# Start of a hybrid decoder block: input requested first, meta tokens over another queue, first query panel by units

## Chip, cores and metric

One core of one Trainium2 chip runs the whole block. The metric is the device time of one execution in microseconds. Three runs of the kernel before took 1568.35, 1568.96 and 1569.6 us.

## The reference, cut to what matters

```python
h = jnp.concatenate([meta, x], axis=1)         # 16 meta tokens + 256 tokens, D_MODEL = 2048
u = rmsnorm(h, attn_norm_w[l])
z = u @ w_in[l]                                # 12368 columns
hq, hf, hi, hg, aq, ak, av, iq, ik, iw, ga, gb = split_cols(z, IN_SIZES)
y_h = hgrn2_mix(hq, hf, hi, hg, lbs[l], hgrn_norm_w[l])
y_a = dsa_mix(aq, ak, av, iq, rmsnorm(ik, idx_k_norm_w[l]), iw, topk)
m = sigmoid(ga) * (y_h @ w_branch_hgrn[l]) + sigmoid(gb) * (y_a @ w_branch_dsa[l])
h = h + m @ w_out[l]
u = rmsnorm(h, ffn_norm_w[l])
a = causal_dwconv(u @ w_ffn_gate[l], ffn_conv_w[l], ffn_conv_b[l])
h = h + (silu(a) * (u @ w_ffn_up[l])) @ w_ffn_down[l]
return rmsnorm(h, final_norm_w)[:, N_META:]
```

All of it is float32.

## The kernel before, in words

Every projection is computed as products of a rounded part (`_hi`) and a remainder (`_lo`): hi x hi, hi x lo and lo x hi. The weights come in panels of 2048 x 256 float32 (2 MB) into two slots, `raw[0]` and `raw[1]`. A panel holds two units of 128 columns. For each unit n ScalarE rounds (`round_unit`, L1241, into `w_hi[n % 4]`, increments `hi_ready`), VectorE subtracts (`rest`, L1569, into `w_lo[n % 4]`, increments `lo_ready`), and TensorE multiplies when `lo_ready` reaches n + 1. SyncE asks for a panel when the remainders of the panel two before are done (`load`). All engines run programs written out by hand, in order, and are tied by semaphores alone.

The change concerns the first 25 us. Unit 0 and 1 are the 80 columns of the indexer's keys and head weights (`KEYS`), units 2 to 9 its queries. In order of the engines:

- SyncE's queue asks for the norm weights (8 KB), the 16 meta rows (128 KB, into partitions 112 to 127 of `x_tok[0]`), then x's left half, the first half of the keys' rows, x's right half, the second half of the keys' rows, the first query panel in two requests of 1 MB (8 of the 16 row blocks each), ten vectors, and the panel of units 4 and 5.
- TensorE warms up on `ones`, turns the norm weights, turns the meta rows (16 transposes, L733), and turns x: 16 column blocks k of two transposes each, into one of seven banks (`turn_x`). The keys' products (L763, L764, L767) run block by block between the turns: `keys_high(k)` waits for `ul_ready` k + 1, `turn_x(k + 7)` follows, and `keys_low(k)` uses `w_lo[0]` once `key_lo` is set (from k = 2 on). Then comes unit 2, in halves: 8 rounded products (L810), 8 products with the remainder (L814), and the rest. Unit 3 follows, with the product that spreads the roots of the token norms (L797, `spread_roots`) after its ninth step and the turn of the vectors after its thirteenth.
- ScalarE squares the meta rows (L1287), rounds the meta tokens' u (L1298), rounds x's turned blocks times the norm weights (`round_x`, L1294), and between the third and fourth of them the first half of the keys (L1302). After the sixteenth it rounds unit 2 in two halves (L1305, L1307; the second waits for the whole panel), rounds unit 3, squares x's first 128 tokens (L1309), and takes the roots (L1311).
- VectorE clears 112 rows of `x_tok[0]` (L1579), weights the turned meta tokens (L1588, four products), and takes the remainders of u (L1601, `rest_x` L1597), with the remainder of the keys' first half between the fourth and fifth (L1605). Then unit 2's remainders (L1609, L1613), unit 3's (L1569), x's second square (L1616), and later the diagonals (L1631) for which L797 waits.
- GpSimd makes `ident`, `ones` and `eps` and does the second half of the keys: rounding L540, remainder L542.

Of the kernel before, what the change touches and what calls it, by code (L numbers as in the profile page):

```python
# [15 lines left out]
F32 = mybir.dt.float32  # L16
F32R = mybir.dt.float32r
ACT = mybir.ActivationFunctionType
# [78 lines left out]
def hybrid_block(nc, x, meta_tokens, attn_norm_w, w_in, hgrn_lb_logits, hgrn_norm_w, idx_k_norm_w,  # L97
# [3 lines left out]
    with ctx:  # L101
# [33 lines left out]
        junk2 = at("junk2", R[0] + 32768, [P, D])  # L135
        vec_rows = at("vec_rows", R[7], [P, 3, P])
        diag = at("diag", R[4] + 6144, [P, 3 * P])
        u_meta = at("u_meta", R[4] + 7680, [P, KT, META])
        x_rs = at("x_rs", R[7] + 7680, [P, T])
# [115 lines left out]
        x_half = [sem(f"x_half{a}") for a in range(2)]  # L255
# [4 lines left out]
        query_in = sem("query_in")  # L260
        key_hi = sem("key_hi")
        key_lo = sem("key_lo")
        meta_turned = sem("meta_turned")
        meta_weighted = sem("meta_weighted")
        meta_rounded = sem("meta_rounded")
# [109 lines left out]
        conv_ready = sem("conv_ready")  # L375
        silu_ready = sem("silu_ready")
        hid_ready = sem("hid_ready")
# [64 lines left out]
        def _(sp):  # L442
# [252 lines left out]
        def _(pe):  # L695
# [29 lines left out]
            pe.wait_ge(consts, 4)  # L725
            warm_up(3)
# [5 lines left out]
            def turn(out, t, k):  # L732
                return nc.tensor.transpose(out, x_tok[t][:, P * k:P * k + P], ident[:])  # L733
# [1343 lines left out]
```

## Time and profile before

| | us |
|---|---|
| median of three runs | 1568.96 |
| lowest, highest | 1568.35, 1569.6 |
| the profiled execution | 1567.8 |
| its span, first to last instruction | 1566.1 |
| TensorE busy | 1554.6 (99%) |
| VectorE busy | 1013.6 (65%) |
| ScalarE busy | 706.1 (45%) |
| GpSimd busy | 141.6 (9%) |
| moved by DMA | 294.62 MB, 188 GB/s on average |

Times in rows are microseconds from the span's start, durations follow. PE is TensorE, DVE VectorE, ACT ScalarE, POOL GpSimd, SP SyncE; a q behind it is its queue. `[0.57 <-DMA x_tok]` behind a row says how long the engine was idle ahead of it and what ended that. Ends of matmuls are modelled, so their starts tell more than their durations.

### The profile page before, as it was taken

The page shows a single profiled execution, that of the slowest core. Times are in us where ns is not written, and L with a number is a line of the kernel's source. Part 1 is how long each engine was busy: PE and PEld are TensorE (multiplying, and loading weights), DVE is VectorE, ACT ScalarE, POOL GpSimd, SP SyncE. Part 2 cuts the span into 40 slices and gives each one's busy share as a digit, 9 for nine tenths or more (in the row PEclk, how much of TensorE's full clock was granted, in tenths as well). Part 3 has the DMA queues.
Part 4 walks back from the last instruction along what each step waited for, and adds up shares of the span by engine and source line. Part 5 has one row for each costly group of instructions (what it writes and reads, how often), then busy time and mean ns, then how long its engine had stood idle before and what let it go on. Part 6 is the DMA issues. An engine that isn't in the chain of part 4 may idle for free.

```text
span 1566.1 us, 28179 instructions
## 1 busy us (share of the span) xinstructions
PE 1554.6 (99%) x11644; PEld 1464.0 (93%) x11644; DVE 1013.6 (65%) x1222; ACT 706.1 (45%) x717; POOL 141.6 (9%) x225
## 2 busy tenths in 40 slices
PE   9999999999999999999999999999999999999998
PEld 7899999999999999999999999998889999998886
DVE  6655888843365666786777777775446777776453
ACT  6433555543433355653445545553333333344342
POOL 1000140000000002247620000000000000000000
PEclk9999999999999999999999999999999999999999
DMA  7765555655565554587877556564556565656551
GB/s 239 231 198 161 161 168 186 197 184 170 184 204 164 162 162 137 180 269 199 231 219 242 190 177 198 161 213 163 213 183 193 173 202 165 203 167 227 177 213 54
DMA packets 264523, 294.62 MB, mean 188 GB/s; under 512 B 23945, under 2 KB 249450, under 8 KB 264306
## 3 DMA queue, kind: packets, MB, share of 16 engines
q1 hardware_dynamic: 238434, 278.78, 54.8%
q0 software_dynamic: 4000, 8.45, 1.9%
q10 hardware_dynamic: 22016, 6.33, 1.7%
q8 instruction: 56, 0.92, 0.2%
q14 instruction: 17, 0.14, 0.0%
HBM read 285.12 MB, written 8.42 MB: 187 GB/s over the span
## 4 chain that ended last, share of the span: by engine, by line
PE 98%; DMA 1%; DVE 1%; SPq 0%; ACT 0%; issue 0%; DVEq 0%
PE ps L701 21%; PE ps L702 20%; PE ps L703 20%; PE ps L1157 10%; PE ps L1199 5%; PE ps L1200 5%; PE ps L1197 5%; PE ps L1155 5%; PE ps L810 2%; PE ps L814 1%; DMA raw<-in_w_in_dram 1%; PE ps L1151 1%; PE ps L901 0%; PE ps L860 0%; PE ps L1021 0%; PE ps L1152 0%
## 5 line engine op out<-in xcount | busy, mean ns | idle before, releaser
L1569 DVE TENSOR_TENSOR w_lo<-raw,w_hi 128x2048 fp32r<-128x2048 f32 x259 | 594.4, 2295 | 310.6 <-ACT w_hi L1241 310.2
L1241 ACT ACTIVATE w_hi<-raw 128x2048 fp32r<-128x2048 f32 x259 | 495.9, 1915 | 546.7 <-PE ps L703 250.8
L701 PE MATMUL ps<-u_all,w_hi 128*128 128x258 f32 (+1 forms) x2112 | 606.0, 287 | 0.0
L702 PE MATMUL ps<-u_all,w_hi 128*128 128x258 f32 (+1 forms) x2112 | 599.7, 284 | 0.0
L703 PE MATMUL ps<-u_all,w_lo 128*128 128x258 f32 (+1 forms) x2112 | 599.1, 284 | 0.0
L701 PEld LDWEIGHTS ps<-u_all,w_hi 128*128 128x128 f32 x2112 | 398.1, 188 | 3.7 <-issue 2.7
L702 PEld LDWEIGHTS ps<-u_all,w_hi 128*128 128x128 f32 x2112 | 398.2, 189 | 1.4
L703 PEld LDWEIGHTS ps<-u_all,w_lo 128*128 128x128 f32 x2112 | 398.2, 189 | 0.0
L1157 PE MATMUL ps<-u_all,w_hi 128*128 128x512 f32 x660 | 233.7, 396 | 0.0
L1155 PE MATMUL ps<-u_all,w_lo 128*128 128x256 f32 x660 | 184.1, 279 | 0.0
L1157 PEld LDWEIGHTS ps<-u_all,w_hi 128*128 128x128 f32 x660 | 123.9, 188 | 27.9
L1200 PE MATMUL ps<-w_lo,hid_hi 128*128 128x512 f32 x352 | 137.0, 389 | 0.0
L1199 PE MATMUL ps<-w_hi,hid_lo 128*128 128x512 f32 x352 | 137.0, 389 | 0.0
L1197 PE MATMUL ps<-w_hi,hid_hi 128*128 128x512 f32 x352 | 136.9, 389 | 0.0
L1155 PEld LDWEIGHTS ps<-u_all,w_lo 128*128 128x128 f32 x660 | 124.7, 189 | 1.9
L1199 PEld LDWEIGHTS ps<-w_hi,hid_lo 128*128 128x128 f32 x352 | 66.1, 188 | 13.8
L1197 PEld LDWEIGHTS ps<-w_hi,hid_hi 128*128 128x128 f32 x352 | 66.1, 188 | 13.8
L1200 PEld LDWEIGHTS ps<-w_lo,hid_hi 128*128 128x128 f32 x352 | 66.1, 188 | 13.5
L703 PE MATMUL ps<-m_hi,w_lo 128*128 128x258 f32 x256 | 72.3, 282 | 0.0
L702 PE MATMUL ps<-m_lo,w_hi 128*128 128x258 f32 x256 | 72.3, 282 | 0.0
L701 PE MATMUL ps<-m_hi,w_hi 128*128 128x258 f32 x256 | 72.3, 282 | 0.0
L1419 ACT ACTIVATE gate_st<-ps 128x258 f32<-128x258 f32 x32 | 12.4, 387 | 92.7 <-PE ps L703 92.7
(320 smaller groups left out, 1654.6 us busy)
## 6 DMA issues: line engine op xcount, KB each, us to landing
raw<-in_w_in_dram SPq DMA_DIRECT2D x47, 2048.0 KB, 8.5
raw<-in_w_ffn_gate_dram SPq DMA_DIRECT2D x22, 2048.0 KB, 8.0
raw<-in_w_ffn_up_dram SPq DMA_DIRECT2D x22, 2048.0 KB, 8.0
raw<-in_w_ffn_down_dram SPq DMA_DIRECT2D x20, 2048.0 KB, 7.8
raw<-in_w_out_dram SPq DMA_DIRECT2D x8, 2048.0 KB, 9.7
raw<-in_w_branch_hgrn_dram SPq DMA_DIRECT2D x8, 1024.0 KB, 5.3
raw<-in_w_branch_dsa_dram SPq DMA_DIRECT2D x8, 1024.0 KB, 8.7
gate_spill<-gate_st ACTq DMA_DIRECT2D x32, 129.0 KB, 3.9
```

What stands on the lines that cost most here:

```text
L701: mm(acc, w_hi[s][:, k, :], mov_hi(k), start=(k == first), stop=False)
L702: mm(acc, w_hi[s][:, k, :], mov_lo(k), start=False, stop=False)
L703: ins = mm(acc, w_lo[s][:, k, :], mov_hi(k), start=False, stop=(k == last))
L810: return mm(ps[n % 2][:].rearrange("p (a t) -> p a t", a=2), w_hi[n % 4][:, k, :], u_all[:, :, k, META:T], start=(k == 0), stop=(k == KT - ...
L814: mm(ps[n % 2][:, 0:SEQ], w_lo[n % 4][:, k, :], u_hi[:, k, META:T], start=False, stop=False, skip_group_check=True)
L1155: mm(acc[:, 0:SEQ], w_lo[s][:, k, :], u2_hi[:, k, 2:TQ], start=False, stop=False, skip_group_check=True)
L1157: ins = mm(both, w_hi[s][:, k, :], u2_all[:, :, k, 2:TQ], start=False, stop=(k == KT - 1), skip_group_check=True)
L1197: mm(acc, hid_hi[:, f, rows], down_hi[s][:, i, :], start=(f == 0), stop=False, skip_group_check=True)
L1199: mm(acc, hid_lo[:, f, rows], down_hi[s][:, i, :], start=False, stop=False, skip_group_check=True)
L1200: ins = mm(acc, hid_hi[:, f, rows], down_lo[s][:, i, :], start=False, stop=(f == FH - 1), skip_group_check=True)
L1241: activation(w_hi[m % 4][:], raw[(m // 2) % 2][:, :, P * (m % 2):P * (m % 2) + P], ACT.Copy)\
L1569: v.tensor_tensor(w_lo[m % 4][:], raw[(m // 2) % 2][:, :, P * (m % 2):P * (m % 2) + P], w_hi[m % 4][:].bitcast(F32), ALU.subtract).then_in ...
```

## The change

SyncE asks for x first: the first two quarters of its columns (0 to 511, 512 to 1023), then the first half of the keys, x's right half, the second half of the keys, unit 2 alone in two requests of 8 row blocks, unit 3 in one, and the meta rows last, ahead of the vectors. The norm weights go to ScalarE's queue, and so do four copies that put the meta tokens as blocks of 32 x 32 into `meta_sh`; VectorE turns them in one instruction and weights them in one more. TensorE's 16 turns of the meta rows go away. GpSimd takes over the clearing of `x_tok[0]` and the remainder of the keys' first half; VectorE fills `ones`. ScalarE rounds the first half of the keys one block later, rounds unit 2's second half when its own request has landed, and squares the meta rows between units 2 and 3. VectorE squares x ahead of unit 3's remainder.

```diff
+        junk3 = at("junk3", R[5] + 4352, [P, D])
+        meta_sh = at("meta_sh", R[6], [P, KT, 32])
+        meta_t = at("meta_t", R[6] + 2048, [P, KT, 32])
...
-            vector(0, V_ATTN, attn_norm_w, 16, norm_in)
-            sp.dma_start(x_tok[0][P - META:P, :], meta_tokens).then_inc(meta_in, 16)
-            for a, done in ((0, key_in), (1, landed[0])):
+            def x_columns(a, c0, c1):
                 for t in range(2):
-                    cols = slice(1024 * a, 1024 * a + 1024)
-                    sp.dma_start(x_tok[1 + t][:, cols], x_rows[:, t, cols]).then_inc(x_half[a], 16)
+                    sp.dma_start(x_tok[1 + t][:, c0:c1], x_rows[:, t, c0:c1]).then_inc(x_cols[a], 16)
+
+            def key_columns(a, done):
                 sp.dma_start(raw[0][:, 8 * a:8 * a + 8, 0:KEYS], w_cols[:, 8 * a:8 * a + 8, C_IK:C_IK + KEYS])\
                   .then_inc(done, 16)
-            for k, done in ((0, query_in), (8, landed[1])):
-                sp.dma_start(raw[1][:, k:k + 8, :], w_cols[:, k:k + 8, C_IQ:C_IQ + 256]).then_inc(done, 16)
+
+            x_columns(0, 0, 512)
+            x_columns(1, 512, 1024)
+            key_columns(0, key_in)
+            x_columns(2, 1024, 2048)
+            key_columns(1, landed[0])
+            for a in range(2):
+                sp.dma_start(raw[1][:, 8 * a:8 * a + 8, 0:P], w_cols[:, 8 * a:8 * a + 8, C_IQ:C_IQ + P])\
+                  .then_inc(query_in[a], 16)
+            sp.dma_start(raw[1][:, :, P:2 * P], w_cols[:, :, C_IQ + P:C_IQ + 2 * P]).then_inc(landed[1], 16)
+            sp.dma_start(x_tok[0][P - META:P, :], meta_tokens).then_inc(meta_in, 16)
...
-            pool.memset(ones[:], 1.0).then_inc(consts, 1)
...
+            pool.memset(x_tok[0][0:P - META, :], 0.0).then_inc(meta_zeroed, 1)
+            pool.wait_ge(key_hi, 1)
+            pool.tensor_tensor(w_lo[0][:, 0:8, 0:KEYS], raw[0][:, 0:8, 0:KEYS], w_hi[0][:, 0:8, 0:KEYS].bitcast(F32),
+                               ALU.subtract).then_inc(key_lo, 1)
...
-            pe.wait_ge(consts, 4)
-            warm_up(3)
+            pe.wait_ge(dve_filled, 1)
+            warm_up(4)
+            pe.wait_ge(consts, 3)
...
-            pe.wait_ge(meta_zeroed, 1)
-            pe.wait_ge(meta_in, 16)
-            for b in range(4):
-                for k in range(4):
-                    ins = turn(ps[b][:, P * k:P * k + P], 0, 4 * b + k)
-                ins.then_inc(meta_turned, 1)
-            pe.wait_ge(norm_ready, 1)
...
-                if 3 <= k < BANKS_X:
-                    pe.wait_ge(meta_weighted, k - 2)
                 if k >= BANKS_X:
                     pe.wait_ge(ul_ready, k - BANKS_X + 1)
-                if k == 8:
-                    pe.wait_ge(x_half[1], 32)
+                if k in (0, 4, 8):
+                    pe.wait_ge(x_cols[k // 4], 32)
+                if k == 2:
+                    pe.wait_ge(norm_ready, 1)
...
+            act.dma_start(vec_rows[V_ATTN:V_ATTN + 16, 0, :], attn_norm_w.rearrange("a (r c) -> (a r) c", c=P))\
+                .then_inc(norm_in, 16)
+            act.wait_ge(dve_filled, 2)
+            for a in range(4):
+                act.dma_start(meta_sh[32 * a:32 * a + META, :, :], meta_blocks[a]).then_inc(meta_sh_in, 16)
+            act.wait_ge(consts, 3)
...
-            act.wait_ge(meta_zeroed, 1)
-            act.wait_ge(meta_in, 16)
-            activation(junk[:], x_tok[0][:], ACT.Square, accum_out=rstat[:, 0:1]).then_inc(x_sum, 1)
...
             for n in range(1, KT + 1):
-                if n == 4:
+                if n == 2:
+                    act.wait_ge(meta_step, 2)
+                    activation(u_hi[:, :, 0:META], u_meta[:], ACT.Copy).then_inc(meta_step, 1)
+                if n == 5:
                     act.wait_ge(key_in, 16)
                     activation(w_hi[0][:, 0:8, 0:KEYS], raw[0][:, 0:8, 0:KEYS], ACT.Copy).then_inc(key_hi, 1)
                 round_x(n)
-            act.wait_ge(query_in, 16)
+            act.wait_ge(query_in[0], 16)
             activation(w_hi[2][:, 0:8, :], raw[1][:, 0:8, 0:P], ACT.Copy).then_inc(hi_half, 1)
+            act.wait_ge(query_in[1], 16)
+            activation(w_hi[2][:, 8:KT, :], raw[1][:, 8:KT, 0:P], ACT.Copy).then_inc(hi_ready, 1)
+            act.wait_ge(meta_zeroed, 1)
+            act.wait_ge(meta_in, 16)
+            activation(junk3[:], x_tok[0][:], ACT.Square, accum_out=rstat[:, 0:1]).then_inc(x_sum, 1)
             act.wait_ge(landed[1], landed_by[1])
-            activation(w_hi[2][:, 8:KT, :], raw[1][:, 8:KT, 0:P], ACT.Copy).then_inc(hi_ready, 1)
             round_unit(3, 3, landed_by[1])
...
+            v.memset(ones[:], 1.0).then_inc(dve_filled, 1)
+            v.memset(meta_sh[:], 0.0).then_inc(dve_filled, 1)
             v.memset(rstat[:], 1.0).then_inc(z_free, 2)
-            v.memset(x_tok[0][0:P - META, :], 0.0).then_inc(meta_zeroed, 1)
...
+            dve.wait_ge(meta_sh_in, 64)
+            v.transpose(meta_t[:].rearrange("p k t -> p (k t)"), meta_sh[:].rearrange("p k t -> p (k t)"))\
+                .then_inc(meta_step, 1)
+            dve.wait_ge(meta_step, 1)
+            v.tensor_tensor(u_meta[:], meta_t[:, :, 0:META],
+                            vec_a[:, V_ATTN:V_ATTN + KT].rearrange("p (k t) -> p k t", t=1).to_broadcast([P, KT, META]),
+                            ALU.mult).then_inc(meta_step, 1)
...
-            dve.wait_ge(meta_rounded, 1)
+            dve.wait_ge(uh_ready, 1)
+            dve.wait_ge(meta_step, 3)
             v.tensor_tensor(u_lo[:, :, 0:META], u_meta[:], u_hi[:, :, 0:META].bitcast(F32), ALU.subtract)
             for n in range(1, KT + 1):
-                if n == 5:
-                    dve.wait_ge(key_hi, 1)
-                    v.tensor_tensor(w_lo[0][:, 0:8, 0:KEYS], raw[0][:, 0:8, 0:KEYS], w_hi[0][:, 0:8, 0:KEYS].bitcast(F32),
-                                    ALU.subtract).then_inc(key_lo, 1)
                 rest_x(n)
...
-            rest(3, 3)
             v.scalar_tensor_tensor(junk2[:], x_tok[2][:], 1.0, x_tok[2][:], ALU.mult, ALU.mult,
                                    accum_out=rstat[:, 2:3]).then_inc(x_sum, 1)
+            rest(3, 3)
```

## Rows read from the trace of the kernel before

**Rows 1.** The chain that ended last, share of the span by engine.

```profile
PE 98%; DMA 1%; DVE 1%; SPq 0%; ACT 0%; issue 0%; DVEq 0%
```

**Rows 2.** TensorE's waits after 12 us: total, times, longest.

```profile
PE ps L797 <- DVE diag L1631: 0.4, 1, 0.4
```

**Rows 3.** Instructions in order of time, TensorE: start, duration, what.

```profile
7.59 1.72 PE L733 MATMUL ps<-ident,x_tok 128*128 128x128 f32 x14 [0.59 <-DMA x_tok<-in_x_dram]
...
9.92 0.35 PE L763 MATMUL ps<-u_all,w_hi 128*80 128x272 f32 x1 [0.61 <-ACT w_hi L1302]
...
10.57 0.29 PE L764 MATMUL ps<-u_all,w_hi 128*80 128x272 f32 x1
11.43 0.41 PE L733 MATMUL ps<-ident,x_tok 128*128 128x128 f32 x2 [0.57 <-DMA x_tok<-in_x_dram]
...
18.69 2.02 PE L810 MATMUL ps<-u_all,w_hi 128*128 128x512 f32 x8
...
24.05 0.63 PE L810 MATMUL ps<-u_all,w_hi 128*128 128x512 f32 x2
...
27.31 0.28 PE L814 MATMUL ps<-u_all,w_lo 128*128 128x256 f32 x1
27.95 0.72 PE L797 MATMUL ps<-diag,ones 128*128 128x272 f32 x2 [0.36 <-DVE diag L1631]
```

**Rows 4.** The same view, SyncE's queue: first request and first request for x.

```profile
0.82 0.39 SPq L445 DMA_DIRECT2D vec_rows<-in_attn_norm_w_dram  x1
...
1.74 0.88 SPq L452 DMA_DIRECT2D x_tok<-in_x_dram  x2
```

**Rows 5.** Tile h_spill (issue ns, landing); DMA queues at 751.5 to 752.0 and 750.0 to 750.5 us.

```profile
L1501 ACTq DMA_DIRECT2D h_spill<-h_sh x64: 309/472/1491, 739.1 to 822.5; - x64
...
DMA to landing us min/median/max: 1.7/5.1/11.1
...
q10 hardware_dynamic: 639, 0.08, 101.8%
...
q1 hardware_dynamic: 153, 0.16, 88.0%
q10 hardware_dynamic: 158, 0.02, 25.4%
```

**Rows 6.** Instructions of the kinds that are moved or added, timeline and tile views.

```profile
1.36 1.76 DVE L1579 MEMSET x_tok<- 112x2048 f32 x1 [0.39 <-issue]
...
L1944 DVE STREAM_TRANSPOSE xm<-xm_sh x1: 711/711/711, 731.8 to 731.8; 128x512 f32<-128x512 f32 x1
...
7.80 0.43 DVE L1601 TENSOR_TENSOR u_all<-u_meta,u_all 128x256 fp32r<-128x256 f32 x1 [0.54 <-ACT u_all L1298]
8.04 1.20 ACT L1294 ACTIVATE u_all<-ps,vec_a 128x256 fp32r<-128x256 f32 x3 [0.27 <-PE ps L733]
9.12 0.74 ACT L1302 ACTIVATE w_hi<-raw 128x640 fp32r<-128x640 f32 x1
...
13.47 1.57 POOL L542 TENSOR_TENSOR w_lo<-raw,w_hi 128x640 fp32r<-128x640 f32 x1
```

**Rows 7.** Timeline, ScalarE and VectorE around units 2 and 3.

```profile
16.54 1.05 ACT L1305 ACTIVATE w_hi<-raw 128x1024 fp32r<-128x1024 f32 x1
...
18.56 1.06 ACT L1307 ACTIVATE w_hi<-raw 128x1024 fp32r<-128x1024 f32 x1 [0.97 <-DMA raw<-in_w_in_dram]
...
21.34 1.90 ACT L1309 ACTIVATE junk<-x_tok 128x2048 f32<-128x2048 f32 x1
21.47 2.29 DVE L1569 TENSOR_TENSOR w_lo<-raw,w_hi 128x2048 fp32r<-128x2048 f32 x1 [0.52 <-ACT w_hi L1241]
...
26.00 0.30 ACT L1311 ACTIVATE rstat<-rstat,eps 128x3 f32<-128x3 f32 x1 [2.68 <-DVE junk L1616]
```

**Rows 8.** Groups by shape, TensorE, 4.3 to 5.6 us and 7.2 to 11 us.

```profile
L733 PE MATMUL ps<-ident,x_tok 128*128 128x128 f32 x6 | 1.5, 420 | 0.0
...
L733 PE MATMUL ps<-ident,x_tok 128*128 128x128 f32 x16 | 2.1, 274 | 0.6 <-DMA x_tok<-in_x_dram 0.6
```

More of the change, by code:

```diff
@@ L254, in hybrid_block @@
         meta_in = sem("meta_in")
-        x_half = [sem(f"x_half{a}") for a in range(2)]
+        dve_filled = sem("dve_filled")
+        meta_sh_in = sem("meta_sh_in")
+        x_cols = [sem(f"x_cols{a}") for a in range(3)]
         norm_in = sem("norm_in")
@@ L259, in hybrid_block @@
         key_in = sem("key_in")
-        query_in = sem("query_in")
+        query_in = [sem(f"query_in{a}") for a in range(2)]
         key_hi = sem("key_hi")
         key_lo = sem("key_lo")
-        meta_turned = sem("meta_turned")
-        meta_weighted = sem("meta_weighted")
-        meta_rounded = sem("meta_rounded")
+        meta_step = sem("meta_step")
         x_sum = sem("x_sum")
@@ L374, in hybrid_block @@
         u2l_ready = sem("u2l_ready")
-        conv_ready = sem("conv_ready")
         silu_ready = sem("silu_ready")
-        hid_ready = sem("hid_ready")
         hidh_ready = sem("hidh_ready")
@@ L729, in _ @@
             warm_up(2)
-            def turn(out, t, k):
-                return nc.tensor.transpose(out, x_tok[t][:, P * k:P * k + P], ident[:])
-            pe.wait_ge(meta_zeroed, 1)
-            pe.wait_ge(meta_in, 16)
-            for b in range(4):
-                for k in range(4):
-                    ins = turn(ps[b][:, P * k:P * k + P], 0, 4 * b + k)
-                ins.then_inc(meta_turned, 1)
-            pe.wait_ge(norm_ready, 1)
             def turn_x(k):
-                if 3 <= k < BANKS_X:
-                    pe.wait_ge(meta_weighted, k - 2)
                 if k >= BANKS_X:
                     pe.wait_ge(ul_ready, k - BANKS_X + 1)
-                if k == 8:
-                    pe.wait_ge(x_half[1], 32)
-                turn(x_bank(k)[:, 0:P], 1, k)
-                turn(x_bank(k)[:, P:2 * P], 2, k).then_inc(x_turned, 1)
-            pe.wait_ge(x_half[0], 32)
+                if k in (0, 4, 8):
+                    pe.wait_ge(x_cols[k // 4], 32)
+                if k == 2:
+                    pe.wait_ge(norm_ready, 1)
+                for t in range(2):
+                    ins = nc.tensor.transpose(x_bank(k)[:, P * t:P * t + P], x_tok[1 + t][:, P * k:P * k + P], ident[:])
+                ins.then_inc(x_turned, 1)
             for k in range(BANKS_X):
@@ L1229, in settle @@
             def settle():
-                act.wait_ge(consts, 4)
+                act.wait_ge(consts, 3)
             def round_unit(n, m, landed_at):
@@ L1278, in loop @@
                         body(i, u, lambda n=n0 + early + per * i + u: ahead(n))
-            act.wait_ge(consts, 4)
+            act.dma_start(vec_rows[V_ATTN:V_ATTN + 16, 0, :], attn_norm_w.rearrange("a (r c) -> (a r) c", c=P))\
[3 more added lines that the diff above has]
+                act.dma_start(meta_sh[32 * a:32 * a + META, :, :], meta_blocks[a]).then_inc(meta_sh_in, 16)
+            act.wait_ge(consts, 3)
             activation(spare[:, 0:1], eps[:], ACT.Sqrt).then_inc(gates_free, 2)
@@ L1295, in round_x @@
                     .then_inc(uh_ready, 1)
-            act.wait_ge(meta_weighted, 4)
-            activation(u_hi[:, :, 0:META], u_meta[:], ACT.Copy).then_inc(meta_rounded, 1)
             for n in range(1, KT + 1):
-                if n == 4:
+                if n == 2:
+                    act.wait_ge(meta_step, 2)
+                    activation(u_hi[:, :, 0:META], u_meta[:], ACT.Copy).then_inc(meta_step, 1)
+                if n == 5:
                     act.wait_ge(key_in, 16)
@@ L1585, in _ @@
             dve.wait_ge(norm_ready, 1)
-            for b in range(4):
-                dve.wait_ge(meta_turned, b + 1)
-                v.tensor_tensor(u_meta[:, 4 * b:4 * b + 4, :],
-                                ps[b][:].rearrange("p (k t) -> p k t", t=P)[:, :, P - META:P],
-                                vec_a[:, V_ATTN + 4 * b:V_ATTN + 4 * b + 4].rearrange("p (k t) -> p k t", t=1)
-                                .to_broadcast([P, 4, META]), ALU.mult).then_inc(meta_weighted, 1)
+            dve.wait_ge(meta_sh_in, 64)
[5 more added lines that the diff above has]
+                            ALU.mult).then_inc(meta_step, 1)
             def rest_x(n):
```

## The prediction

> **What bounds the kernel now.** I read the chain that ended last first, then TensorE's waits, then the order in time of the first 30 us. The chain is 98% TensorE [rows 1], and after 12 us the waits of TensorE hold one entry, of 0.4 us, at L797 [rows 2]: behind it TensorE works through to the end with no gap. So only the moment at which TensorE passes the roots' product (L797, at 27.95 us, unit 3) matters; each microsecond by which it comes earlier or later moves the end by one. In front of it the rows show four points [rows 3]. The turns of x begin at 7.59 us, when the first half has landed. The keys' first product waits for its weights until 9.92. The ninth turn waits for the second half of x until 11.43. From there TensorE is full: 7.26 us later, at 18.69, unit 2 starts, unit 3 starts at 24.28 (0.23 us into the row of two at 24.05), and nine of its steps end at 27.43 (0.12 behind the start of the row at 27.31; 3.15 us, 0.35 a step), where L797 stands 0.52 us for VectorE's diagonals. What limits today is thus, in this order, x's second half, then TensorE itself, then the diagonals.
>
> **x first, by column quarters.** The first request for x leaves at 1.74 us now; it moves to the place of the first one, 0.82 us [rows 4]: 0.92 us earlier. The last columns, in at 11.3 us today (TensorE goes on at 11.43), would be in at 10.4. Against this stand four small copies over ScalarE's queue, 1024 pieces of 128 B, 64 for each DMA engine. The nearest row is h_spill, also 128 B pieces on that queue: with the queue alone 639 of them take 101.8% of 16 engines over half a microsecond, 12.7 ns each [rows 5]. 64 x 12.7 ns = 0.81 us for each engine; the 131 kB in long rows that stood ahead of x take 131 kB / 320 GB/s = 0.41 us (320 GB/s from the row of 153 packets, 0.16 MB in 0.5 us [rows 5]). Net 0.40 us later: x complete at 10.8. It may be as early as 10.4 if they fill gaps. The Trainium skill (DMA: Bandwidth & Descriptors, Specifications) puts the line rate at pieces of 512 B and more; taken as if these pieces were no worse than others, the sum would have 10.4, and the row sides with the page's rule.
>
> **Meta tokens over ScalarE's queue, turned by VectorE.** Gone from TensorE are 16 turns; they ran while it waited for x, so they give nothing. Gone from VectorE are four small products, and a memset of 112x2048 that took 1.76 us [rows 6] goes to GpSimd, which is idle then. New, one behind the other: VectorE clears meta_sh (512 of that memset's 2048 columns: 0.44 us, ready at about 1.6), ScalarE issues four copies at 0.31 to 0.47 us each [rows 5], done at about 3.3; its table load then fits before the first turn of x is ready. Landing after an issue took from 1.7 to 11.1 us with a median of 5.1 in the same rows, the longer ones behind a 2 MB load of weights. Here x stands in the way. In the pair at 750 us the two queues take turns one for one (153 against 158 packets [rows 5]), so the 64 small pieces of each engine pass while x's quarters (16 pieces each) and half of the first key panel pass; that is about 1.3 MB of traffic. The bounds for all of them landed, M, are 5.0 us (3.3 + 1.7) and 8.4 (3.3 + 5.1), with 14.4 (the 11.1) as the far end that needs a load in front; I take M = 7.0, where that traffic is through.
> From M: VectorE turns 128x512 (0.71), scales (0.43), ScalarE rounds (0.42 by the same shape), rounds x three times (1.20) and the first key panel (0.74), with four hand-overs of 0.03 to 0.1: M + 3.6 = 10.6 us [rows 6]. VectorE's own first remainder of x comes at M + 2.1 and runs at 0.48 a piece, ahead of TensorE's need. So the keys' first product moves from 9.92 to 10.6. Queued behind VectorE's new wait is every remainder of x, and behind those TensorE's turns from the eighth on.
>
> **Keys.** From 9.92 to 18.69 are 8.77 us with about 0.74 of waiting for x in them (the ninth turn's), so 8.03 of work. The panel's remainder moves from VectorE (0.82) to GpSimd: 1.57 us by its sister instruction L542 [rows 6]. TensorE asks for it after three steps of 0.51 us, so it waits 0.1. GpSimd's work on the second half of the keys starts when that lands, as now, and has an unchanged 1.5 us and more before TensorE asks for it. Unit 2 starts at the later of 10.6 + 8.03 + 0.1 = 18.7 and 10.8 + 7.26 = 18.1. I take 18.7: no gain, against 18.69. The 0.8 us that VectorE is spared lie beside TensorE's work.
>
> **First query panel by units.** The halves needed first are asked for first. Today ScalarE's second rounding of unit 2 waits for the whole panel until 18.56; its first ended at 17.6 [rows 7]. Both halves of unit 2 are now as many bytes as today's first request, which was there in time at 16.54, so the second rounding can end at 18.65. Unit 2 itself had no wait today [rows 2] and gains nothing. Unit 3's weights would come 1 us earlier, if nothing was put between.
>
> **The square of the meta rows goes in there.** It stood ahead of x's roundings in idle time; now ScalarE does it between unit 2's and unit 3's rounding, after a wait for the 128 KB meta rows, which are now the last piece in SyncE's queue before the vectors. What was the panel's landing, 18.5 us, is moved 0.92 us forward by x and backwards by 0.41 (131 kB that are read twice now), 0.40 (small pieces) and some 0.2 (pieces of 512 instead of 1024 B; bounds 0 and 1): 18.6, with hand-over 18.7. The bounds are 18.0 and 19.5. Then square with its read 1.98, rounding of unit 3 1.94, and VectorE's remainder 2.29: ready at 24.9, where today it is ready at 23.76 and wanted at 24.28 [rows 7]. Unit 3 starts at 24.95, 0.67 us late. Queued behind ScalarE's wait are unit 3's and 4's rounding and x's second square.
>
> **What that square's move buys.** VectorE's square of x goes ahead of unit 3's remainder, done at 22.4 instead of 25.97; ScalarE's ends at 24.4. The roots then come at 24.5 instead of 26.0, the diagonals by 26.4 instead of 27.9: the 0.52 us wait goes. What is late next is unit 3 itself.
> The roots' product: 24.95 + 9 x 0.35 = 28.1, against 27.95: **0.15 us later**. From there on ScalarE's and VectorE's chain over unit 4's rounding is about 1.3 us earlier than now, while TensorE is not, so no later unit, none of which waits today, loses room. Everything behind stays the same.
>
> **Sum.** The profiled execution took 1567.8 us, 1566.1 of span and 1.7 around it. 1567.8 + 0.15 = 1567.95. The median of the runs shown is 1.16 above that execution, so 1568.96 + 0.15 = **1569.1**. A measurement of this kernel tells 0.2%, or 3.1 us, from no change.
>
> **Rivals.**
> (a) A small gain. If the small copies are in by 6 us and the meta rows by 18.0, unit 2 starts at 18.1 and L797 at 18.1 + 1.98 + 1.94 + 2.29 + 3.15 = 27.46, 0.5 us earlier: 1568.5. Since the meta rows are last in the queue they can hardly be in before 17.6, so 0.9 us is the most there is: 1568.1. For it: x moves first. Against: ScalarE and SyncE issue at once, and copies slowed each other at 745 us (up to 1.49 us an issue).
> (b) Slower: the wait for meta_sh in front of all of VectorE's remainders. It decides from M = 7.0 on; each microsecond is one at the end. With the median landing of 5.1, M = 8.4 and unit 2 at 20.1: 1.5 us later, 1570.5. The far end, M = 14.4, gives 7.5 us, 1576.5; nothing here puts a load in front.
> (c) TensorE's clock. Every window grants 1.00, the 2.4 GHz level, yet a turn takes 420 ns at 4.3 to 5.6 us and 274 after 7.2 [rows 8]: a slower pace from its first product at 1.61 on, for about 3.9 us of nearly unbroken work. Now its work has a gap from about 4.0 to the first quarter at 5.2 and one of 2 us ahead of the keys at 10.6. If it then runs at half pace for another 3.9 us, the keys take 1.95 longer: unit 2 at 20.65, ScalarE's rounding with it, 1571.0. Against: three gaps of 0.6 us [rows 3] did not bring it back. The Trainium skill (TensorE: Matmul & The Clock Gate, Part 1) says that the gate halves the clock after idleness; the slow turns at the start agree, and no row here shows a fall.
> (d) The change doesn't do what it says: SyncE's six requests, interleaved with ScalarE's, bring x no sooner (11.3 + 0.4). Unit 2 starts at 19.0, 1569.4.
>
> **Numbers.** Forecast with (d) 0.50, (a) 0.22, (b) 0.14, (c) 0.11, something else 0.03. Only the far end of (b), or (b) and (c) together, reach 3.1 us. Faster by over 0.2% 0.03, within 0.2% 0.91, slower 0.06. The range reaches from (a)'s bound less the spread of the runs (0.6) to (c) with a bit of (b): 1567.3 to 1571.4.
>
> **What would show it.** In the profile after: x's last columns land near 10.8; the stream transpose starts near 7; L763 first at about 10.6; unit 2 at 18.7; ScalarE's rounding of unit 3 starts near 20.7, and TensorE waits for VectorE's w_lo ahead of unit 3; no wait at L797. It is wrong if TensorE shows no wait for unit 3 (then the square was covered), or shows waits after 28 us.

## The result and the profile after

The changed kernel takes **1575.34 us** (median of 6 runs, 1574.16 to 1576.04), the kernel before 1569.17 (6 runs beside them, 1568.35 to 1569.6): ratio 1.0039, 95% interval 1.0028 to 1.0049, 6.2 us slower. Its profiled execution took 1574.67, with a span of 1572.8 where before has 1566.1: 6.7 more. I forecast 1569.1, no change.

In the first 30 us the chain of work that ended last is no longer TensorE's. This is the changed kernel's (start, us, what), to be read against [rows 1]; q1 is SyncE's queue and q10 ScalarE's in all views below:

```profile
1.66 0.69 ACTq L1287
2.39 0.63 ACTq L1287
3.05 0.63 ACTq L1287
3.71 8.34 DMA meta_sh<-in_meta_tokens_dram
12.15 0.72 DVE meta_t L1597
13.77 1.09 ACT u_all L1298 x3
14.86 0.63 ACT w_hi L1307
15.54 0.51 PE ps L765
...
22.95 1.05 ACT w_hi L1310
24.01 0.95 ACT w_hi L1312
24.95 1.89 ACT junk L1315 x2
26.84 1.82 ACT w_hi L1243
28.69 2.30 DVE w_lo L1578
31.04 0.50 PE ps L812
```

One transfer holds 8.3 us of it: the last of the four small copies of the meta tokens. The tile view of `meta_sh` has all four (issue ns, landing), and answers to the first line of [rows 5]:

```profile
L1287 ACTq DMA_DIRECT2D meta_sh<-in_meta_tokens_dram x4: 629/632/692, 1.7 to 3.7; - x4
...
DMA to landing us min/median/max: 5.0/6.2/8.3
```

TensorE in order of time answers to [rows 3]: turns of x, first product of the keys, turns after it, unit 2, the roots' product.

```profile
7.66 1.36 PE L754 MATMUL ps<-ident,x_tok 128*128 128x128 f32 x6 [0.52 <-DMA x_tok<-in_x_dram]
...
15.54 0.51 PE L765 MATMUL ps<-u_all,w_hi 128*80 128x272 f32 x1 [6.52 <-ACT w_hi L1307]
...
16.95 0.63 PE L754 MATMUL ps<-ident,x_tok 128*128 128x128 f32 x2
...
25.11 2.02 PE L812 MATMUL ps<-u_all,w_hi 128*128 128x512 f32 x8
...
34.28 0.62 PE L799 MATMUL ps<-diag,ones 128*128 128x272 f32 x2
```

The roots' product starts at 34.28, not 27.95: 6.33 us later. That is 5.62 at the keys' first product (15.54 against 9.92) and 0.80 in the keys (9.57 us against 8.77, though 0.74 of waiting has gone from them), less 0.09 in units 2 and 3. The windows show why the keys are slower. Each row has the stretch, its length, the busy time of PE, PEld, DVE, ACT and POOL, then the granted clock as a share of 2.4 GHz, the DMA share and GB/s:

```profile
9.00:12.00 3.00, 0.02 (x1) 0.00 (x0) 0.00 (x0) 0.00 (x0) 0.00 (x0) 1.00 1.12 327
12.00:19.00 7.00, 3.46 (x16) 3.46 (x17) 5.37 (x12) 4.64 (x11) 3.29 (x3) 0.51 1.20 295
19.00:25.00 6.00, 6.00 (x52) 6.00 (x51) 4.35 (x8) 4.79 (x9) 0.48 (x1) 1.00 0.80 218
```

TensorE stood still for 6.5 us; its grant then fell to the 1.2 GHz level from 12 to 19 us, and two turns take 0.63 us there instead of 0.38.

Two smaller things happen later. TensorE's waits after 20 us hold two entries where [rows 2] has one:

```profile
PE ps L1068 <- DVE probs L1913: 1.1, 1, 1.1
PE ps L812 <- DVE w_lo L1578: 0.2, 1, 0.2
```

The first is at the last attention head. A small VectorE instruction there, 128x2 on `stat` (called the stat instruction below), takes 2.40 us beside GpSimd's multiplies of four gate tiles. In the kernel before it takes 1.25 and nobody waits. Changed kernel, then before:

```profile
630.77 4.64 POOL L642 TENSOR_TENSOR gates<-gates,x_rs 128x516 f32<-128x516 f32 x4
...
633.04 2.40 DVE L1854 TENSOR_SCALAR stat<-stat 128x2 f32<-128x2 f32 x1
```

```profile
627.47 1.25 DVE L1846 TENSOR_SCALAR stat<-stat 128x2 f32<-128x2 f32 x1
```

It ends 2.27 + 2.40 = 4.67 us behind the start of GpSimd's row in the one, 2.26 + 1.25 = 3.51 in the other (GpSimd starts at 625.21): with the fourth and with the third of four multiplies of 1.16 us. The Trainium skill (SBUF — State Buffer, Who interferes with whom) has VectorE and GpSimd share one pair of ports as an exclusive lock for a whole instruction; the whole multiples of 1.16 agree with it. Why the instruction, ready 0.05 us before the second multiply ends, gets through only behind the third or the fourth is not shown.

In return, three short stalls of the kernel before are gone. Two of them are these rows of its timeline:

```profile
31.28 0.85 PE L810 MATMUL ps<-u_all,w_hi 128*128 128x512 f32 x2
...
44.33 0.89 PE L810 MATMUL ps<-u_all,w_hi 128*128 128x512 f32 x2
```

An undisturbed row of two takes 0.63 [rows 3]. With the 0.10 inside L797's own row (0.72 against 0.62) that is 0.58 us which the "no gap" of my prediction passed over, since the waits view doesn't list so short a stop. The changed kernel needs 0.76 us less for the whole stretch from the roots' product to the last head; the other 0.18 I have not placed.

### The profile page after: what moved, and what is told of

It is laid out like the page before. It is cut to its first block, busy times and chain, and to the rows that moved or that the text cites. A ratio compares the mean times of both kernels' runs of the same rounds, so it can differ in the third digit from the quotient of the medians.

```text
span 1572.8 us, 28157 instructions
## 1 busy us (share of the span) xinstructions
PE 1554.8 (99%) x11630; PEld 1464.6 (93%) x11630; DVE 1015.3 (65%) x1220; ACT 706.2 (45%) x717; POOL 144.6 (9%) x226
## 4 chain that ended last, share of the span: by engine, by line
PE 98%; DVE 1%; ACT 1%; DMA 1%; ACTq 0%; issue 0%; DVEq 0%
PE ps L713 20%; PE ps L714 20%; PE ps L715 20%; PE ps L1159 10%; PE ps L1201 5%; PE ps L1202 5%; PE ps L1199 5%; PE ps L1157 5%; PE ps L812 2%; PE ps L816 1%; PE ps L1153 1%; DMA meta_sh<-in_meta_tokens_dram 1%; PE ps L903 0%; PE ps L862 0%; PE ps L1023 0%; PE ps L1154 0%
## 5 line engine op out<-in xcount | busy, mean ns | idle before, releaser
L1201 PEld LDWEIGHTS ps<-w_hi,hid_lo 128*128 128x128 f32 x352 | 66.1, 188 | 13.8
L1199 PEld LDWEIGHTS ps<-w_hi,hid_hi 128*128 128x128 f32 x352 | 66.1, 188 | 13.8
```

What stands on the lines that cost most here:

```text
L1199: mm(acc, hid_hi[:, f, rows], down_hi[s][:, i, :], start=(f == 0), stop=False, skip_group_check=True)
L1201: mm(acc, hid_lo[:, f, rows], down_hi[s][:, i, :], start=False, stop=False, skip_group_check=True)
```

## The experiments

Milestones of every profiled execution, in us: the keys' first product, unit 2, the roots' product; then the stretch from there to GpSimd's copy of `p_rows` at the last head, and from that to the end of the span. Medians and ratios are of the timed runs.

| kernel | keys | unit 2 | roots | to last head | to the end | median | ratio to before |
|---|---|---|---|---|---|---|---|
| before | 9.92 | 18.69 | 27.95 | 597.11 | 941.04 | 1569.17 | |
| changed | 15.54 | 25.11 | 34.28 | 596.35 | 942.17 | 1575.34 | 1.0039 [1.0028, 1.0049] |
| e1_big_pieces | 12.46 | 22.90 | 32.07 | 596.52 | 942.21 | 1572.61 | 1.0020 [1.0011, 1.0030] |
| e2_kept_busy | 16.39 | 24.64 | 33.81 | 596.53 | 942.16 | 1574.67 | 1.0033 [1.0021, 1.0044] |
| e3_only_meta_path | 15.52 | 25.07 | 33.81 | 596.35 | 942.14 | 1574.42 | 1.0032 [1.0019, 1.0045] |
| e4_turned_by_pe | 12.91 | 21.16 | 30.34 | 596.32 | 942.14 | 1570.53 | 1.0008 [0.9998, 1.0018] |
| e5_copies_on_sync | 11.86 | 22.74 | 32.80 | 596.53 | 942.17 | 1573.43 | 1.0027 [1.0017, 1.0036] |
| e6_before_again | 10.18 | 18.89 | 28.11 | 597.12 | 941.07 | 1568.04 (one) | |
| e7_pe_square_early | 12.94 | 21.18 | 30.19 | 596.52 | 942.19 | 1570.50 | 1.0004 [0.9995, 1.0013] |
| e8_squares_act_gates_held | 10.58 | 18.81 | 27.55 | 596.50 | 941.85 | 1568.02 | 0.9991 [0.9982, 1.0000] |
| e9_gates_held | 11.53 | 20.97 | 29.87 | 597.26 | 941.87 | 1569.14 | 0.9998 [0.9989, 1.0007] |
| e10_after_gates_held | 15.25 | 25.05 | 34.22 | 596.53 | 941.85 | 1575.40 | 1.0037 [1.0023, 1.0051] |
| e11_x_quarters_only | 11.16 | 19.39 | 28.13 | 596.52 | 941.85 | 1568.42 | 0.9993 [0.9984, 1.0002] |
| e12_squares_act | 10.36 | 18.64 | 27.38 | 596.67 | 942.15 | 1568.41 | 0.9996 [0.9987, 1.0005] |

### The four copies in big pieces

```diff
-                act.dma_start(meta_sh[32 * a:32 * a + META, :, :], meta_blocks[a])
+                act.dma_start(meta_sh[32 * a:32 * a + META, :, :].rearrange("p k t -> p (k t)"),
+                              meta_tokens[:, 512 * a:512 * a + 512])
```

> The four copies into meta_sh bring the same 128 KB in rows of 2 KB (16 pieces a copy instead of 256), so the meta tokens stand in the wrong order there; all else is the changed kernel. Theory P (the 128-byte pieces, 64 on each DMA engine, take turns one for one with SyncE's pieces, and only therefore land at 12.1 us): 4 pieces an engine are through by about 6 us, VectorE's turn starts at 5.5 to 6.5, the keys' first product near 9.5 to 10 instead of 15.5, no half pace of TensorE, and the time falls by 5 to 6 us, to about that of the kernel before (1569 to 1570). Rival Q (ScalarE's queue is served late while SyncE's is full, whatever the pieces are): the turn still starts near 12, the time stays at 1575.

The features of the meta tokens stand in another order here, so what this kernel leaves out is their right order, and it serves for its times alone. The issues fall from 0.63 to 0.44 us and the stream transpose starts at 9.07 instead of 12.15, unit 2 at 22.90, 2.7 us off the median. In the tile view of `meta_sh`:

```profile
L1287 ACTq DMA_DIRECT2D meta_sh<-in_meta_tokens_dram x4: 373/442/443, 1.7 to 3.0; - x4
...
DMA to landing us min/median/max: 3.5/4.4/6.0
```

Neither theory came: the transpose was forecast for 5.5 to 6.5 or for 12. The size and number of the pieces are about half of the lateness. The other half stays, and a strict one-for-one turn does not explain it. With 64 pieces in all there are 4 for each engine, yet they land up to 6.0 us after their issue. From 5 to 6 us, in this run:

```profile
q1 hardware_dynamic: 138, 0.24, 81.6%
q10 hardware_dynamic: 29, 0.03, 12.4%
```

### TensorE kept busy in the gap

```diff
             for k in range(BANKS_X):
                 turn_x(k)
+            warm_up(28)
```

> The changed kernel with 28 idle products on ones (56 passes) behind the first seven turns of x, so that TensorE has work from 9 us until the keys' weights are there. Theory C (the half pace from 15.5 to 18.9 us comes from TensorE's idleness before it): the granted clock stays 1.00 in the window of 10 to 20 us, the keys take 8.1 instead of 9.6 us from their first product to unit 2, which starts near 23.6 instead of 25.1, 1.5 us off the time: 1573.9. Rival: the clock fell for another reason, then nothing changes; if the extra products themselves are late (they end after 15.5), up to 1 us is lost.

The granted clock of 10 to 20 us is 1.00 (0.66 in the changed kernel) and the keys take 8.25 us instead of 9.57. But the small copies came 0.85 us later in this execution, so that only 0.5 of the 1.3 us shows at the roots' product, and the median is 0.7 lower, where 1.4 was expected, inside both intervals. The lower clock follows from the wait for the meta tokens and costs 1.3 us of the 6.3; it isn't what makes them late.

### The meta tokens' path alone, on the kernel before

```diff
+            act.wait_ge(dve_filled, 1)
+            for a in range(4):
+                act.dma_start(meta_sh[32 * a:32 * a + META, :, :], meta_blocks[a]).then_inc(meta_sh_in, 16)
...
-            for b in range(4):
-                for k in range(4):
-                    ins = turn(ps[b][:, P * k:P * k + P], 0, 4 * b + k)
-                ins.then_inc(meta_turned, 1)
...
+            dve.wait_ge(meta_sh_in, 64)
+            v.transpose(meta_t[:].rearrange("p k t -> p (k t)"), meta_sh[:].rearrange("p k t -> p (k t)"))\
+                .then_inc(meta_step, 1)
```

> The kernel before with one part of the change alone: four copies over ScalarE's queue into meta_sh, VectorE's turn and one product, no turns of the meta rows by TensorE (the 128 KB row copy for the square stays first). Theory P: the copies land near 12 here too, the keys start near 15.5 and the time is 5 to 6.5 us over the kernel before, 1574 to 1575.5. Rival R (the other parts together cost most of it: order of requests, 512-byte pieces, the square between the units): at most 2 us over the kernel before.

With x, the keys and the queries asked for as before, this part by itself makes 1574.42 us, 5.3 of the 6.2, inside Theory P's range. The stream transpose starts at 12.28. The turns of x's left half start at 8.50 instead of 7.59, but an execution of the kernel before without small copies (e9_gates_held) has 8.72 too, so it isn't shown that the copies slow x.

### The meta tokens turned by TensorE again

The four copies are one request of the 16 rows on ScalarE's queue, behind the norm weights; the 16 turns and four products are back; the rest is the changed kernel.

```diff
-            for a in range(4):
-                act.dma_start(meta_sh[32 * a:32 * a + META, :, :], meta_blocks[a]).then_inc(meta_sh_in, 16)
+            act.dma_start(x_tok[0][P - META:P, :], meta_tokens).then_inc(meta_in, 16)
```

> The changed kernel with the meta path of before: one request of 128 KB in 8 KB rows behind the norm weights on ScalarE's queue, 16 turns by TensorE, four small products; all other parts of the change stay. Theory P: keys start near 9.5, unit 2 between 17.8 and 18.4, then the square between units 2 and 3 makes TensorE wait for unit 3; L797's counterpart at 27.2 to 28.0, the time within 1 us of the kernel before (1568.3 to 1569.5). Rival R: the time stays over 1572, since order, pieces and square cost it.

1570.53: 4.8 us of the 6.2 are gone, though it is 1.0 us above Theory P's range. What is left, 1.4 us with an interval that holds no change, stands ahead of unit 2. From the timeline:

```profile
6.33 3.65 PE L746 MATMUL ps<-ident,x_tok 128*128 128x128 f32 x16 [1.35 <-DMA x_tok<-in_meta_tokens_dram]
```

16 rows in long pieces on ScalarE's queue need 4.9 us from issue to use (the chain has them from 1.27 on), beside x on SyncE's queue. Before, ahead of x in SyncE's own queue, they landed 2.7 us after an issue at 1.27 and their turns started at 4.42. The 16 turns also take 3.65 us here, where before they took 2.58.

### The copies on SyncE's queue

```diff
             x_columns(0, 0, 512)
+            sp.wait_ge(dve_filled, 2)
+            for a in range(4):
+                sp.dma_start(meta_sh[32 * a:32 * a + META, :, :], meta_blocks[a]).then_inc(meta_sh_in, 16)
```

> The changed kernel with its four small copies asked for by SyncE, between x's first and second column quarter, and so in one queue with x; nothing else moves. Theory Q (a copy on ScalarE's queue comes late because SyncE's queue is served beside it, whatever the pieces): behind only 256 KB of x in the same queue the 1024 pieces are through by 6.5 to 7.5 us; the stream transpose starts there (12.15 in the changed kernel), the keys' first product 3.4 us behind it, at 10 to 11, unless x's right half, now behind the small pieces, is what it waits for; unit 2 at 19 to 20.5 (25.11), the roots' product at 28.5 to 30 and the time 1570 to 1571. Theory P (128-byte pieces are slow in themselves): 64 pieces for each engine take as long as before, the transpose starts at 9 or later, x's later quarters are held up by 2 us and more, unit 2 at 22 or later, 1572.5 or more.

The landing is near Theory Q's: the same 1024 pieces of 128 B are in at 6.45 us, 2.5 to 3.2 us behind their issues (ahead of them stand both requests of x's first quarter, 512 KB and not the 256 of the expectation):

```profile
L459 SPq DMA_DIRECT2D meta_sh<-in_meta_tokens_dram x4: 598/608/702, 1.7 to 3.8; - x4
...
DMA to landing us min/median/max: 2.5/2.6/3.2
```

The queues' view (packets, MB, share of 16 engines) of 4 to 5 us in this run, where the pieces pass, and of 9 to 10 us in the changed kernel, where both queues are at work and 99 pieces of q1, of some 3.6 KB each, pass beside 100 of q10. Behind them is the changed kernel's 5 to 6 us:

```profile
q1 hardware_dynamic: 691, 0.11, 59.7%
```

```profile
q1 hardware_dynamic: 99, 0.36, 96.2%
q10 hardware_dynamic: 100, 0.01, 8.9%
```

```profile
q1 hardware_dynamic: 142, 0.26, 72.5%
q10 hardware_dynamic: 233, 0.03, 18.5%
```

So the pieces cost little themselves (59.7% of 16 us over 691: 13.8 ns, [rows 5] gave 12.7) and land late beside a full queue. How the two queues share an engine is not settled: one for one holds from 8 to 10 us, not at 5 to 6, where 233 small pieces pass beside 142, nor at 3 to 4, where 4 pass beside 117. This run also changes two things at once, the queue of the copies and how much SyncE has asked for while they pass (its next request leaves at 4.41 us). Small copies on ScalarE's queue with SyncE held back were not run, so it isn't shown which of the two makes them quick.

The time came out 2.4 us above the upper end that Theory Q gave, in Theory P's range, though not for Theory P's reason: four issues of 0.6 us now stand in front of x, its second quarter is in at 9.06, the keys' weights at 11.07, and a clock of 0.66 in 10 to 20 us and a wait of 1.1 for unit 3 follow. The wait moved from the meta tokens to x; putting the copies elsewhere does not save this path.

### The kernel before, profiled again

> The kernel before, profiled a second time. In every profile of the changed kernel and of the experiments so far VectorE's small TENSOR_SCALAR on stat at the last attention head, at about 633 us, takes 2.40 us while GpSimd multiplies four gate tiles, and TensorE then waits 1.1 us; in the one profile of the kernel before it takes 1.25 us and TensorE does not wait. Theory L (it hangs on the phase between the engines and differs from execution to execution): this profile shows 2.4 us and a wait of about 1 us, and a profiled execution of about 1569, at the median. Theory N (the kernel before never has it): 1.25 us again, no wait, about 1568.

The instruction takes 1.25 us again, and 941.07 us follow to the end. Theory N came in both profiles of this kernel. They lie 1.1 and 1.4 us below the median of its runs all the same, and some of the next runs ask why.

### The square of the meta rows early again

```diff
             act.wait_ge(z_free, 2)
+            act.wait_ge(meta_zeroed, 1)
+            act.wait_ge(meta_in, 16)
+            activation(junk3[:], x_tok[0][:], ACT.Square, accum_out=rstat[:, 0:1]).then_inc(x_sum, 1)
             act.wait_ge(norm_ready, 1)
```

> The fourth run's kernel (changed kernel, meta rows as one request and turned by TensorE) with the square of the meta rows on ScalarE back at its old early place, ahead of the roundings of x, where ScalarE waits anyway. Theory S (what is left over the kernel before, 1.4 us, is the square between units 2 and 3 and a bit of lateness before unit 2): no wait ahead of unit 3 (0.2 before), the roots' product again 0.2 to 0.4 us earlier than 30.34, near 30.0, 1570.1 to 1570.3. Rival T: the place of the square costs nothing, since the lateness arises ahead of unit 2 (21.16 against 18.69): 1570.5, and the gap ahead of unit 3 is filled by a wait elsewhere.

The wait ahead of unit 3 goes and the roots' product is 0.15 earlier, but the median stays (1570.50 against 1570.53), as Rival T said. The square's place costs 0.15 us in the profiles and nothing that the medians can tell.

### Both squares of x on ScalarE, gates held

```diff
             activation(junk[:], x_tok[1][:], ACT.Square, accum_out=rstat[:, 1:2]).then_inc(x_sum, 1)
+            activation(junk2[:], x_tok[2][:], ACT.Square, accum_out=rstat[:, 2:3]).then_inc(x_sum, 1)
...
+            pool.wait_ge(p_ready, 8)
             for n in range(4):
                 scale_gates(n, 16)
```

VectorE's `scalar_tensor_tensor` on `x_tok[2]` is gone.

> The kernel before with two edits elsewhere: VectorE's square of x's second 128 tokens goes to ScalarE, behind its own, so that VectorE is free after unit 3's remainder; and GpSimd's first four gate multiplies wait until VectorE has made the last head's probabilities. If the waits seen in front of the roots' product (0.52 us) and at the last attention head (1.1 us in the profiles where VectorE's stat instruction takes 2.4) are both real and both go, TensorE shows no wait after 12 us and the time is 1567.0 to 1568.2. If the gates come late then (GpSimd needs 4.6 us for them and ScalarE asks for the first at about 641 us), TensorE waits there and nothing is won: 1569 or more. If the first wait moves to unit 4 or 6, which need ScalarE, 1568.5 to 1569.

1568.02 is the lowest median of all, inside the range; the ratio is 0.9991 and its interval reaches 1.0000, so no gain is proved. The roots' product has no wait and starts at 27.55. The stat instruction falls to 0.17 us.

```profile
626.46 0.17 DVE L1846 TENSOR_SCALAR stat<-stat 128x2 f32<-128x2 f32 x1
...
628.56 6.92 POOL L630 TENSOR_TENSOR gates<-gates,x_rs 128x516 f32<-128x516 f32 x4 [4.34 <-DVE probs L1905]
```

GpSimd's four multiplies take 6.92 instead of 4.64 us in their new place, and TensorE waits 0.2 for a gate. Span against span this run is only 0.2 us shorter than the kernel before (1565.9 against 1566.1), since both profiles of that kernel were quick ones; the profiles don't explain the 1.2 us between the medians.

### The held gates alone, before and after

> The kernel before with one edit: GpSimd's first four gate multiplies wait until VectorE has made the last head's probabilities. Both profiles of the kernel before show VectorE's stat instruction there at 1.25 us and no wait of TensorE, yet lie 1.1 to 1.4 us below the median of its runs. Theory G (in its unprofiled runs the instruction often takes the long 2.4 us and TensorE waits 1.1): the median falls to about 1568.1 and the runs lie closer together than the 1567.5 to 1571.2 of before, and the squares, the other edit of the eighth run, were worth nothing. Rival H (profiled executions are just quicker, and the eighth run's gain is the wait at the roots' product): 1568.9 to 1569.3 and the same spread.

> The changed kernel with the same one edit. Its profile shows the 2.40 us and the 1.1 us wait that the kernel before doesn't have. Theory G: the wait goes from the profile (span 1571.7, from 1572.8) and the median falls by about as much as it does for the kernel before, to 1574.2 to 1574.4, so that the change costs the same with and without it. Rival K (the changed kernel always has the wait, the kernel before never): here the median falls by the full 1.1 us, to 1574.2, and in the ninth run it does not fall, so that the wait is part of the cost of the change.

Neither median moves by what its interval can tell, so Theory G falls, and the 1574.2 that both theories gave for the changed kernel did not come (1575.40). The stretch from the last head to the end is 941.85 to 941.87 us with the gates held, 942.14 to 942.21 with the long instruction, and 941.04 and 941.07 in the two profiles of the kernel before. Holding the gates thus wins only 0.3 of the 1.1 us; where the other 0.8 goes is open. Rival H gave the right time for the kernel before, but not for its reason: the profiled execution here was the slowest of its eleven runs. It shows one thing that spreads the runs of this kernel: the landing of x.

```profile
PE ps L734 <- DMA x_tok<-in_x_dram: 3.3, 2, 2.1
```

This execution took 1570.69, and its first half of x was used from 8.72 us on, where [rows 3] has 7.59.

### What of the change could stay

The eighth run's kernel with the norm weights on ScalarE's queue and x's right half in two quarters:

```diff
-                    sp.dma_start(x_tok[1 + t][:, cols], x_rows[:, t, cols]).then_inc(x_half[a], 16)
+                for c in ((0, 1024),) if a == 0 else ((1024, 1536), (1536, 2048)):
...
+                if k in (8, 12):
+                    pe.wait_ge(x_half[k // 4 - 1], 32)
```

> The eighth run's kernel (kernel before, both squares of x on ScalarE, gates held) with the part of the change that its trace did not speak against: the norm weights over ScalarE's queue, so that SyncE's first request is the meta rows, and x's right half in two column quarters, the thirteenth turn waiting for the second. x should land 0.4 us earlier and the ninth turn go on after the first quarter: unit 2 at 18.1 to 18.4 (18.81), 1567.4 to 1567.8. Rival: the norm weights land 3 us after their issue on ScalarE's queue, as in the changed kernel, but are wanted only after the meta turns; no loss by them; if the keys' first half is what TensorE waits for, as in the eighth run (0.9 us), nothing is won: 1568.0.

The eighth run's kernel is not beaten: 1568.42 (1568.19 to 1568.74), where 1567.4 to 1567.8 was expected. The norm weights hold TensorE 0.5 us, the meta turns start at 4.99 instead of 4.42, and the keys' first product at 11.16 instead of 10.58. TensorE has no wait for x, as in the eighth run's profile.

### The squares alone

> The kernel before with one edit: x's second square goes from VectorE to ScalarE, behind its own, so that VectorE is free for unit 4's and unit 5's remainders earlier. The eighth run (this and the held gates) was 1.2 us under before and the ninth (held gates alone) 0.3 us. Theory V (the eighth run's gain is this edit: TensorE's waits at the roots' product, 0.4 us, and the short one at unit 6 go): 1568.0 to 1568.5, no wait of TensorE between 12 and 600 us. Rival: the two edits need each other, since earlier work on VectorE meets GpSimd's gate multiplies in another phase and gets the long 2.4 us there: 1.1 us wait at the last head, about 1569.2.

Theory V holds at the start: there is no wait at the roots' product, which starts at 27.38. The rival holds at the end: the stat instruction takes 2.40 us and TensorE waits 1.1. The median is 1568.41, 0.85 below before, with an interval that holds no change. At the last head this edit changes nothing but the moment at which the engines arrive (GpSimd copies `p_rows` at 624.05, before at 625.06), and it gets the long instruction, which the kernel before does not. What decides between the third and the fourth multiply is open.

## Why the prediction was wrong

- **The step that failed** is "I take M = 7.0", the landing of the four small copies. They landed at 12.1. The issues were put at 0.31 to 0.47 us each from [rows 5] and took 0.63, so they were done at 4.3 instead of 3.3. The landing was put at 3.7 us behind the end of the last issue and took 7.7 (8.3 from its start). I let the 64 small pieces of each engine pass one for one with SyncE's, from their issue on, through "about 1.3 MB of traffic". In the trace ScalarE's queue passed 88 pieces up to 5 us, those of the norm weights among them, while SyncE's passed 391, the bulk (707) only from 5 to 8, and the last 325 took until 12.05. The ratio of the two queues is near one in two windows of ten. Experiment 5 shows the same pieces in at 6.45 while SyncE asked for little else, experiment 1 shows 9.07 with a sixteenth of the pieces, and experiment 4 a late landing on that queue with long ones. What sets the share of the second queue stays open.
- **A second step failed behind it**, and M hid it. x was to be complete at 10.8. The last request for x, on SyncE's queue, with its median us from issue to landing, changed kernel, then before:

```profile
x_tok<-in_x_dram SPq DMA_DIRECT2D x1, 512.0 KB, 8.2
```

```profile
x_tok<-in_x_dram SPq DMA_DIRECT2D x1, 512.0 KB, 7.4
```

From issues at 4.0 and 3.9 us these are 12.2 and 11.3: x came 0.9 us later, not 0.5 earlier. The 0.92 us that x's first request gained did not reach the right half, because asking for the left half in quarters takes four requests instead of two: the right half is asked for from 3.17 us on, before from 3.14. Even in experiment 4, without the small pieces, it was in at 11.7, which is what rival (d) put (11.3 + 0.4). By the prediction's own 7.26 us from x's landing to unit 2, a landing at 12.2 puts unit 2 at 19.5 or later, an estimate, even with M = 7.0.
- **From M to the keys' first product the sum was right**: M + 3.6 was forecast, and 12.15 + 3.4 = 15.54 came. The keys behind it took 9.57 us and not the 8.1 of the forecast, at the lower clock of rival (c).
- **Rival (b)** is what happened. M came 3.7 us beyond its median bound and 2.3 short of its far end. I gave it 0.14, since "nothing here puts a load in front". SyncE's requests for x, the keys and the queries were such a load. Its rule, one us per us from M = 7.0, gives 5.1 of the 6.33.
- **Rival (c)** came with it: the grant did fall to the lower level, 12 to 19 us, after 6.5 us without work. I priced it at 1.95; experiment 2 gives 1.3 (keys in 8.25 us at the full clock, 9.57 without). The Trainium skill (TensorE: Matmul & The Clock Gate, Part 1), which speaks of a clock halved after idleness, agrees with these rows.
- **x first** did what was said for its first quarters (turned from 5.22 and 7.66), and that bought nothing, as forecast: TensorE stopped when the seven banks were full.
- **Norm weights** I moved at no cost. They were used at 4.02 instead of 3.19, again after a landing on ScalarE's queue. The wait for x hid that here; in experiment 11 it held TensorE for 0.5 us.
- **Queries by units** I priced at 0.2 us. In pieces of 512 B SyncE's queue moves 0.29 MB in a microsecond where 1 KB pieces moved 0.35: 12 to 13 us, changed kernel, then before.

```profile
q1 hardware_dynamic: 587, 0.29, 119.2%
```

```profile
q1 hardware_dynamic: 344, 0.35, 110.5%
```

The panel's 2.1 MB take 7.2 instead of 6.0 us that way. Nothing waited for them here. The rule of 512 B that I cited (the Trainium skill, DMA: Bandwidth & Descriptors, Specifications) puts these at the line rate; in these rows they are 17% under pieces twice as long.
- **The meta rows' square** was put at 0.67 us ahead of unit 3. TensorE waited 0.2 there, because ScalarE's rounding of unit 2, no longer waiting for its request, ended at 24.95, before unit 2 began.
- **"no later unit, none of which waits today, loses room"** missed 0.58 us of short stalls and 1.1 us at the last head. The stretch to the last head is shorter both in experiment 3, which starts it late (596.35 us), and in experiment 12, which only moves x's second square off VectorE (596.67, before 597.11). I did not look beyond 30 us, and there GpSimd's multiplies hold up VectorE.

The account: 6.33 at the roots' product, less 0.76 to the last head, and 1.13 from there, make 6.7 us of span. The medians differ by 6.2, since the profiled execution of the kernel before was 1.4 us below its median and that of the changed kernel 0.7. The wait for the meta tokens is shown as the cause of some 5 us by experiments 3 and 4.

## What to carry to other kernels

A small transfer on a second queue was not small here while the first queue was full: 128 KB needed 5.0 to 8.3 us from issue to landing in 1024 pieces and 3.5 to 6.0 in 64. Fewer, longer pieces helped, but no count of pieces gave the time, so take such a landing from a trace of the same load, and look at what is queued behind it before anything else. Count requests too: splitting early ones in two pushes every later one back, and for x's right half that used up all that asking for x first had gained. Of the arrangements tried, the quickest asked for the operand that everything waits for first in the busy queue, in few long pieces, and let an engine turn it; the 16 turns ran while TensorE would have waited for x, and the transfer that replaced them cost some 5 us. When a chain shows 98% of one engine, ask which other engine's work is just under it, and look for rows a quarter of a microsecond too long, which no list of waits has.

## What the runs showed of the hardware

- 1024 pieces of 128 B in SyncE's queue, with no other queue at work, take 13.8 ns of an engine each and land 2.5 to 3.2 us behind their issues (experiment 5). On ScalarE's queue beside a full queue of SyncE's they land after 5.0 to 8.3 us.
- The time of an issue depends on the pieces: about 0.63 us for 256 pieces of 128 B on either queue (up to 0.85 in experiment 3), 0.44 for 16 of 2 KB.
- One VectorE instruction of 128x2 takes 0.17 us with GpSimd's four multiplies of 1.16 us held back. Beside them it takes 1.25 us, when it ends with the third of them, or 2.40, when it ends with the fourth. Held until VectorE has made the probabilities, the four multiplies take 6.92 us instead of 4.64.
- The granted clock fell to the 1.2 GHz level after TensorE had stood still from 9.0 us on, and came back at about 19 us, when it had worked again since 15.54. In experiment 2, with filler products in the gap, it was 1.00 in every window of the first 30 us.
